# Where the split weights stand in SBUF against the activations, in phases that move 256 columns: 224 and 160 bytes in place of 192

## What is computed

```python
# first_block: two layers on x (256 tokens) and, beside it, a context z (256 tokens)
x = ffn_sublayer(x, mx, 0, g[0], g[1], ffn_w_gu[i, 0], ffn_w_down[i, 0])   # z too
# layer 0: short convolution of x and z; layer 1: window attention, x over x and z
x = adaln_out(x, yx, g[3], mx[5], 1.0)
x = ffn_sublayer(x, mx, 6, g[4], g[5], ffn_w_gu[i, 1], ffn_w_down[i, 1])   # z in layer 0

def swiglu(h, w_gu, w_down):                    # D_FF = 2816
    gu = h @ w_gu
    return (jax.nn.silu(gu[..., :D_FF]) * gu[..., D_FF:]) @ w_down

# second_block, x alone
proj = rms_norm(x, g_mix[i]) @ w_in[i]          # queries, keys, values, gates
# two attention mixers on proj, then
x = x + merged @ w_out[i]
x = x + (jax.nn.silu(gate) * up) @ w_ffn_out[i]
x = x + ple_gate * (p[i] @ w_ple_proj[i])
```

## Time and profile before

| what | us |
|---|---|
| time, median of 3 runs (2172.98 to 2177.02) | 2176.26 |
| the profiled execution, its own time | 2176.27 |
| its span, from the first to the last instruction | 2174.7 |
| outside the span (2176.27 - 2174.7) | 1.6 |
| TensorE busy with matmuls, of the span | 2091.3 |
| VectorE busy | 1529.4 |
| ScalarE busy | 1043.1 |

### The profile page before, as it was taken

One profiled execution on the slowest core, in us unless ns is written; L12 is line 12 of the kernel. 1 busy time (PEld: TensorE's weight loads), 2 busy tenths in 40 slices (PEclk: granted clock), 3 DMA queues, 4 the chain that ended last, 5 costly groups with the idle time before them and its releaser, 6 DMA issues. The chain is left out here.

```text
span 2174.7 us, 35166 instructions
## 1 busy us (share of the span) xinstructions
PE 2091.3 (96%) x14546; PEld 1892.2 (87%) x14546; DVE 1529.4 (70%) x2435; ACT 1043.1 (48%) x1675; POOL 90.8 (4%) x67
## 2 busy tenths in 40 slices
PE   5999999999899999999999999998999899999998
PEld 4988889998899888899988889868999787799998
DVE  3666776886885667778566777886666676777666
ACT  5622223763584232358423236675444444655444
POOL 1000000000110000010000001001000101000000
PEclk9999999999999999999999999999999999999999
DMA  7555555455445455455555545403455542245554
GB/s 308 191 174 197 198 184 179 166 191 194 157 175 186 171 203 194 167 190 178 197 174 208 193 161 186 172 1 129 169 203 174 207 153 78 79 162 188 200 185 143
DMA packets 70014, 378.76 MB, mean 174 GB/s; under 512 B 7392, under 2 KB 12384, under 8 KB 42976
## 3 DMA queue, kind: packets, MB, share of 16 engines
q1 hardware_dynamic: 66960, 369.92, 48.3%
q10 hardware_dynamic: 2896, 6.60, 0.9%
HBM read 375.45 MB, written 1.05 MB: 173 GB/s over the span
## 5 line engine op out<-in xcount | busy, mean ns | idle before, releaser
L588 PE MATMUL ps_g<-h,w_hi 128*128 128x256 f32 (+2 forms) x4288 | 976.4, 323 | 15.0 <-DVE h L1077 7.5
L972 DVE TENSOR_TENSOR w_lo<-w_raw,w_hi 128x1024 fp32r<-128x1024 f32 (+2 forms) x614 | 691.4, 1129 | 349.1 <-ACT w_hi L1567 347.8
L1567 ACT ACTIVATE w_hi<-w_raw 128x1024 fp32r<-128x1024 f32 (+2 forms) x614 | 590.4, 968 | 564.6 <-PE ps_g L588 385.0
L588 PEld LDWEIGHTS ps_g<-h,w_hi 128*128 128x128 f32 x4288 | 716.0, 189 | 82.2 <-issue 15.3
L588 PE MATMUL ps_g<-h,w_lo 128*128 128x256 f32 (+2 forms) x2144 | 690.4, 322 | 0.0
L588 PE MATMUL ps_g<-hid,w_hi 128*128 128x256 f32 (+1 forms) x2368 | 479.4, 302 | 7.1 <-DVE y L1144 4.5
L588 PEld LDWEIGHTS ps_g<-h,w_lo 128*128 128x128 f32 x2144 | 406.8, 190 | 31.6
L588 PEld LDWEIGHTS ps_g<-hid,w_hi 128*128 128x128 f32 x2368 | 377.0, 188 | 30.8 <-issue 4.4
L588 PE MATMUL ps_g<-hid,w_lo 128*128 128x256 f32 (+1 forms) x1184 | 355.7, 300 | 0.0
L588 PE MATMUL ps_g<-b_h,w_hi 128*128 128x256 f32 x1504 | 269.9, 283 | 10.5 <-DVE b_h L1077 7.4
L588 PEld LDWEIGHTS ps_g<-b_h,w_hi 128*128 128x128 f32 x1504 | 230.6, 191 | 18.5 <-issue 17.1
(11 more groups left out here) (274 smaller groups left out, 1592.0 us busy)
## 6 DMA issues: line engine op xcount, KB each, us to landing
w_raw<-in_gu SPq DMA_DIRECT2D x130, 1024.0 KB, 4.8
mod_raw<-in_w_mod SPq DMA_DIRECT2D x128, 512.0 KB, 3.6
w_raw<-in_conv_cu SPq DMA_DIRECT2D x16, 1024.0 KB, 4.8
w_raw<-in_dn00b SPq DMA_DIRECT2D x16, 768.0 KB, 4.2
w_raw<-in_dn01b SPq DMA_DIRECT2D x16, 768.0 KB, 4.1
w_raw<-in_dn10b SPq DMA_DIRECT2D x16, 768.0 KB, 4.2
w_raw<-in_conv_out SPq DMA_DIRECT2D x8, 1024.0 KB, 4.8
w_raw<-in_w_in_a SPq DMA_DIRECT2D x8, 1024.0 KB, 5.0
```

What stands on the lines that cost most here:

```text
L588: mm = pe.matmul(at, w[wp][:, k, m * P:(m + 1) * P], acts[ap][:, k, cs], start=(k == 0 and n == 0 and not (one_bank and m)), stop=(k == kc ...
L972: dve.tensor_tensor(lo_of(u)[:, cols], w_raw[u % 2][:, cols], hi_of(u)[:, cols].bitcast(F32), ALU.subtract).then_inc(lo_made, 1)
L1567: act.activation(hi_of(u)[:, cols], w_raw[u % 2][:, cols], ACT.Copy).then_inc(hi_made, 1)
```

## The change

The slot of the weights is no longer 80 words for all phases off the 512-column ones. It is 72 words (288 bytes) for units of the first two layers, `conv_b` included, and 88 words (352 bytes) for units of the second block. The activations then stand 512 - 288 = 224 bytes past the weights in the first two layers and 512 - 352 = 160 bytes past them in the second block. The phases on 512 columns keep distance 0. The spare room of the buffers is dealt out anew so that all tiles from `x` on keep their addresses.

```diff
 def weight_slot(u):
 
-    return 0 if UNITS[u].cols == BOTH and UNITS[u].phase != "conv_b" else 80
-
-
-HI_STARTS, LO_STARTS = (0, 80), (48, 0)
+    if UNITS[u].cols == BOTH and UNITS[u].phase != "conv_b":
+        return 0
+    return 72 if u < FIRST["w_in_a"] else 88
+
+
+HI_STARTS, LO_STARTS = (0, 88), (72, 0)
...
-    w_hi = [sb(f"w_hi{j}", [P, UNIT + (80, 96)[j]], F32R) for j in range(2)]
-    w_lo = [sb(f"w_lo{j}", [P, UNIT + 80], F32R) for j in range(2)]
-    sb("fill0", [P, 32])
+    w_hi = [sb(f"w_hi{j}", [P, UNIT + (88, 112)[j]], F32R) for j in range(2)]
+    w_lo = [sb(f"w_lo{j}", [P, UNIT + (56, 88)[j]], F32R) for j in range(2)]
+    sb("fill0", [P, 24])
```

## The result

The changed kernel is slower. Its median is 2187.38 us (5 runs, 2181.78 to 2193.61) against 2176.26 for the kernel before (2168.23 to 2184.02 in the runs made beside it). The ratio is 1.0053 with a 95% interval of 1.0033 to 1.0073. The forecast was 2162.7 us, so its sign is wrong; the time lies within the range of 2152 to 2190.

What follows compares the result with a forecast made beforehand. It took TensorE's matmul rate as the bound. From 2176.27 us, gains of 8.8, 2.4, 1.3 and 1.1 us, together 13.6, gave 2162.7 us, with a range for 8 in 10 of 2152 to 2190.

Steps and rivals of the forecast that it cites:

- The two spacings: 256-column matmuls at distance 192 start every 113.3 or 117.8 ns, 3.9% apart; settled after a wait, then kept.
- What the new distances do: At 224 and 160 bytes, matmul and weight load were to settle in the short rhythm; forecast's chance 0.46.
- step 1: First two layers, 192 to 224 bytes: gains of 8.8, 2.4 and, in `conv_b`, 1.3 us; `gu3` taken as nothing.
- The 8.8 us: Gain in the first layers from 1972 long-spaced matmuls becoming short, 4.44 ns each.
- The 2.4 us for the broken phases: First-layer phases broken by waits: 1100 matmuls taken as long, worth 4.9 us, half of it reaching the end.
- Step 2: Second block, 192 to 160 bytes: nothing to win from 1962 us on, 1.1 us from 238 long matmuls in `w_in_a`.
- What was priced as a possible loss: Short matmuls turning long: 2832 in the first layers, 12.6 us, and 2546 in the second block, 11.3 us.
- Step 3: ACT, DVE and three waits: unit 13's copy starts up to 2.55 us earlier without gain; DVE's low part stays 1224 ns.
- The next limit: Whether a faster TensorE meets another limit: the 8.8 us were held covered, the gain in the down phases was halved.
- the slower rival: 256-column weight loads lengthen or only the long rhythm is left: 23.9 us more, 2200 us; one block 2188 to 2189; chance 0.22.
- Placement without a part: Rival: matmul and weight load read without touching, addresses do not matter, time 2176.3 us; chance 0.05.
- The redraw: Rival: both spacings persist at the new distances and each wait picks one, 2170 to 2182 us; chance 0.27.

Runs made afterwards that it cites:

- e9: The kernel before, unchanged, run again for a second profile: 2176.24 us.
- e11: Kernel before with distance 0 in the first two layers, `conv_b` included, and 384 bytes in the second block: 2193.09 us, one execution.
- e4: Kernel before with distance 64 bytes in the first two layers and 320 in the second block: 2183.39 us, one execution.
- e16: The changed kernel, unedited, timed and profiled again: 2187.63 us, ratio 1.0056 to the kernel before.
- e7: Kernel before with its own distance in most phases, 192 bytes elsewhere (512 columns included), tiles from `x` on 256 bytes up: 2217.21 us, one execution.
- e5: Changed kernel with the second block back at 192 bytes, first layers still at 224: 2186.31 us, ratio 1.0049 to the kernel before.
- e8: Kernel before with tiles from the raw weights on 32 bytes up and low-part buffers placed like the high-part ones: 2170.10 us, ratio 0.9971.

## Why the prediction was wrong

**The two spacings.** Right, and it is the key to the result. e9 confirms that a stretch gets either one at the same addresses, and that it is drawn anew in each execution, as the earlier trace rows had suggested for two places in one trace.

**What the new distances do.** This is the step that failed: that a step off the 64-byte grid "has a fair chance to break the long one". It breaks the short one, and it puts a slightly longer one, 118.3, in the place of 117.8. `gu2az` went from 113.3 to 118.5 ns and `gu4b` from 113.3 to 117.2. The reason given was that the short spacing appears at both distances seen, at 192 and, doubled, at 0. But the 226.7 ns at 0 belonged to matmuls of 512 columns, and e11 shows 256 columns at 0 taking 120.1. The trace of before had 256 columns at 192 bytes and, in the few matmuls of `token_unit`, at 320, both odd multiples of 64. It could not say what another distance does, and the text had said so; yet it gave the gain 0.46 and the loss 0.22 on an analogy across sizes.

**The terms of step 1.** The 8.8 us in the five long stretches of the first layers became a small loss: 117.8 to 118.3, 0.5 ns on 1972 matmuls, 1.0 us. The 2.4 us for the broken phases went with it. `conv_b` kept 233.5 ns, where 226.7 was assumed; e4 shows that its spacing does depend on the distance (229.5 at 64), but 224 is not better than 192. `gu3` was put at nothing and had 0.7 ns less on 1056 matmuls, 0.7 us, a spacing that 192 bytes has in some executions too.

**Step 2.** Nothing to win, as said, and 65 us of `gu4b` hold 557 matmuls where they held 576.

**What was priced as a possible loss.** The prediction named 12.6 us in the first layers and 11.3 in the second block, and left them out of its sum. TensorE's busy time up to `w_in_a` grew by 10.5 us in the first profile and 13.2 in e16, behind it by 5.9 and 7.6. So the first figure was near and the second too high, also when the 1.5 us of the clock are added to the 5.9.

**Step 3.** Right. The copy for unit 13 started at 107.17 us where it had started at 111.24, earlier by more than `gu0az` ended earlier, and nothing followed from it. DVE's low part takes 1225 ns at slot 72 against 1224. ACT in order of time, first profile of the change:

```profile
107.17 1.05 ACT L1569 ACTIVATE w_hi<-w_raw 128x1024 fp32r<-128x1024 f32 x1
109.78 0.38 ACT L1716 ACTIVATE gate_tmp<-ps_g 128x256 f32<-128x256 f32 x1 [1.56 <-PE ps_g L590]
```

**The next limit.** The prediction halved the gain in phases broken by waits. The same holds for a loss, and it was not applied to the slower rival, which was priced at 23.9 us of matmuls, 2200 us. TensorE's busy time did grow by 16.4 and 20.8 us. The span grew by 5.5 and 11.6 only, because 10.9 and 9.2 us of TensorE's waiting disappeared. That the time lies inside the stated range is luck: the range took in a loss in one block at its full price and left out a loss in both, and what came was a loss in both at about half the price.

**The rivals.** The slower one was right in its second form, "only the long rhythm is left", and wrong in its first: loads stayed at 188 ns while matmuls went to 280 and 281. Of its two marks, 281 ns in `gu4b` came (280), and loads over 188 ns did not. Its reason, that the load decides as soon as it exceeds 113.3 ns, can't be had from the rows: a load of 188 ns goes with a spacing of 113.3, so the loads overlap in the trace, and PEld busy in 65.00 of 65.00 us doesn't show that they have no slack. Placement without a part is out: all kernels issue the same matmuls on the same data, and the spacing goes from 113.3 to 123.6 ns with the distance alone. The Trainium skill, in "TensorE: Matmul & The Clock Gate", section "Step-by-step: what each phase is for", says that a weight load takes no SBUF read bandwidth from the running matmul since the two have separate read ports. The measurement decides against the strong reading, that placement can't matter, at least for this float32 format: how far the two operands stand from each other matters by up to 9%. Whether they meet in SBUF or on the way from it, no run tells. The redraw is real for the kernel before, whose runs reach from 2165 to 2185 us, but does not bridge the gap, since none of the changed kernel's three profiles has a stretch with the short spacing.

## What to carry to other kernels

Where two spacings exist for one instruction, a change of address can take away either, and only a run at that address and that very size tells which. Before moving a tile, measure one kernel with a distance of its own in each phase, as e7 does: one execution can hold a dozen. And read the gain or loss of a busy engine together with its waits; here 9.2 of 20.8 us and 10.9 of 16.4 came back from them. Where a spacing is drawn anew in each execution, compare the draws before comparing the times: one long draw of some 1500 matmuls at an unchanged distance made up 5.1 of e5's 11.5 us.

## What the runs showed of the hardware

- A 256-column matmul of this format, alternating with weight loads, has a spacing that depends on the distance of the two operands modulo 512 bytes. Of the 21 distances tried only the odd multiples of 64 allow 113.3 ns. The others take 117 to 124, the worst being 208 bytes, 16 from the best.
- With 512 columns the order is another one: 0 is best (226.7), 64 takes 229.5, 192 and 224 take 233.5. With 258 columns 64 bytes was best (118.7), and 192 took 120.0 or 120.8.
- At an odd multiple of 64 the spacing has two values, 113.3 or 117.8 ns, for the same instructions on the same addresses. Which one a stretch gets differs between executions of one program.
- A TensorE that had idled for 2.37 us was granted half the clock for the next 3 us, and one that had idled for 0.41 us was not. One that had idled for 2.08 us was too (e8), and one that had idled for 2.58 us was not (e11), so something beside the length of the wait plays a part.
